# A hybrid decoder layer on one Trainium2 core: probabilities of the sliding attention folded to one square per head, scores on quarters of the array, both attentions in common visits

## The reference: what is computed

```
cb, cc, ch, cz, q, k, v, sz, mq, mz = project_in(x, pre_g, w_in)
u = cc * ch
y_conv = cb * short_conv(u_full, conv_w) * silu(cz)           # 3 taps, 384 channels
y_swa  = swa_attention(q, k_band, v_band, ...) * silu(sz)     # 6 heads, 2 kv heads, dim 64
y_mem  = mem_attention(mq, mk, mv) * silu(mz)                 # 4 heads, 256 memory tokens
y = x + rms_norm(concatenate([y_conv, y_swa, y_mem]) @ w_out, post_g)
```

## Time and profile before

| | us |
|---|---|
| median of 3 runs | 930.3 (930.17 to 930.33) |
| profiled execution | 930.49 |
| its span, first to last instruction | 928.7 |
| PE matmul busy | 890.9 (96%) |
| DVE busy | 472.8 (51%) |
| POOL busy | 485.5 (52%) |
| ACT busy | 269.0 (29%) |

### The profile page before, as it was taken

How to read it: one execution, slowest core, us unless ns; L and a number is a source line. 1 busy time by engine, 2 the same in 40 slices (tenths; PEclk the granted TensorE clock), 3 DMA queues, 4 the chain that set the end, 5 groups by cost and what they waited for, 6 DMA issues and landing times.

```text
span 928.7 us, 12297 instructions
## 1 busy us (share of the span) xinstructions
PE 890.9 (96%) x4846; PEld 717.0 (77%) x4846; DVE 472.8 (51%) x891; ACT 269.0 (29%) x726; POOL 485.5 (52%) x279
## 2 busy tenths in 40 slices
PE   1899999999999999999999999999999999999995
PEld 1799999897887777777787777777777777777784
DVE  3443247667543544674736444765535225576413
ACT  4333433331311342432311333422221124323111
POOL 1557644418667444446658444454556754444560
PEclk9999999999999999999999999999999999999998
DMA  9443421215465232212747322211822622122232
GB/s 345 182 137 125 152 70 66 69 47 196 169 200 208 99 107 91 68 68 72 268 139 267 116 91 91 68 68 48 290 76 69 216 69 78 62 75 81 84 121 90
DMA packets 40106, 114.64 MB, mean 123 GB/s; under 512 B 6001, under 2 KB 12657, under 8 KB 39633
## 3 DMA queue, kind: packets, MB, share of 16 engines
q1 hardware_dynamic: 40048, 113.86, 35.3%
HBM read 104.61 MB, written 10.25 MB: 124 GB/s over the span
## 4 chain that ended last, share of the span: by engine, by line
PE 72%; issue 2%; DVE 1%; DMA 0%; POOL 0%; POOLq 0%; DVEq 0%
PE pj L520 50%; PE pa L520 18%; PE pa L617 2%; PE pa L654 1%; DMA x_t<-in_xt 0%; DVE o_nat L1342 0%; POOL w_lo L492 0%; DVE diag L1057 0%; PE pa L541 0%; POOLq L196 0%; DVEq L196 0%; POOL w_hi L491 0%; PE pa L590 0%; PE pa L569 0%; DVE k_sb L1313 0%
## 5 line engine op out<-in xcount | busy, mean ns | idle before, releaser
L520 PE MATMUL pj<-h_hi,w_hi 128*128 128x512 f32 (+1 forms) x960 | 348.2, 363 | 1.8 <-DVE h_lo L1077 1.7
L520 PE MATMUL pj<-h_lo,w_hi 128*128 128x512 f32 (+1 forms) x960 | 339.1, 353 | 0.0
L520 PE MATMUL pj<-h_hi,w_lo 128*128 128x512 f32 (+1 forms) x960 | 338.7, 353 | 0.0
L492 POOL TENSOR_TENSOR w_lo<-w_raw,w_hi 128x1024 fp32r<-128x1024 f32 x132 | 329.2, 2494 | 11.0
L491 POOL TENSOR_SCALAR w_hi<-w_raw 128x1024 fp32r<-128x1024 f32 x132 | 146.8, 1112 | 328.1 <-PE pj L520 279.6
L520 PEld LDWEIGHTS pj<-h_hi,w_hi 128*128 128x128 f32 x960 | 181.7, 189 | 49.6 <-issue 23.7
L520 PEld LDWEIGHTS pj<-h_hi,w_lo 128*128 128x128 f32 x960 | 181.9, 190 | 24.9
L520 PEld LDWEIGHTS pj<-h_lo,w_hi 128*128 128x128 f32 x960 | 182.1, 190 | 22.5
L918 ACT ACTIVATE prob<-s_sb,nmx 128x257 f32<-128x257 f32 x96 | 47.7, 502 | 56.2 <-DVE nmx L1256 56.2
L520 PE MATMUL pa<-w_hi,y_hi 128*128 128x512 f32 x160 | 63.5, 397 | 0.0
L520 PE MATMUL pa<-w_hi,y_lo 128*128 128x512 f32 x160 | 62.4, 390 | 0.0
(11 more groups left out here) (188 smaller groups left out, 1070.3 us busy)
## 6 DMA issues: line engine op xcount, KB each, us to landing
w_raw<-in_weights SPq DMA_DIRECT2D x132, 512.0 KB, 3.3
res<-in_x_prompt SPq DMA_DIRECT2D x16, 512.0 KB, 6.8
out_y_prompt<-o_nat SPq DMA_DIRECT2D x16, 512.0 KB, 5.7
x_row<-in_x_prompt SPq DMA_DIRECT2D x12, 512.0 KB, 3.4
x_t<-in_xt SPq DMA_DIRECT2D x12, 512.0 KB, 5.4
first_rows<-in_x_prompt SPq DMA_DIRECT2D x4, 512.0 KB, 5.6
x_t<-in_xt SPq DMA_DIRECT2D x8, 256.0 KB, 5.4
mkt_s<-in_mkt SPq DMA_DIRECT2D x2, 1024.0 KB, 5.6
```

The costliest lines, as they stand in the source:

```text
L492: pool.tensor_tensor(w_lo[slot][:], w_raw[slot][:], w_hi[slot][:].bitcast(F32), ALU.subtract).then_inc(w_split, 1)
L520: return pe.matmul(out, lhsT, rhs, start=start, stop=stop)
```

## The change

- **Fold.** Of the two 128 x 128 squares of a head's probabilities (block before, own block) the masked half is zero, and the halves complement each other. `swa_norm` adds the two squares and multiplies the sum (128 columns per head) by the reciprocal. `swa_turn` then makes one transpose per head. `swa_pt` moves to DVE and multiplies each turned square by two triangular masks `seen`, a new constant of 128 x 2 x 128, loaded with the other constants; this gives `pt` its two squares again.
- **Quarters.** `swa_scores` makes two matmuls per head, each for 64 queries, on one quarter (64 rows, 64 columns) of the array, and with the 192 keys that these queries can see at most. `mem_scores` makes two per head and block too, with all 256 keys. Two PSUM banks are set to zero at the start, since parts of them are now read before they are written.
- **Common visits.** One table `ATT_S` for both scores and one `ATT_V` for both values; the transposes come 8 and 9 parts after the scores, the values 13. `swa_norm` and `mem_norm` stand at 3 and 4 parts after. M0 and M1 move up in `ROLES`, the memory tiles in quarter 0 too, and the sample's stages are earlier and closer together.
- The first gate of a quarter waits for `y_rows`, which DVE itself has counted up before.

```diff
-ROLES = ["V0", "K0", "Q0", "Q1", "Q2", "Z0", "Z1", "Z2", "M0", "M1", "Z3", "Z4"]
+ROLES = ["V0", "K0", "Q0", "Q1", "Q2", "M0", "Z0", "Z1", "Z2", "Z3", "M1", "Z4"]
...
-    return ROLES[:8] + MEM_TILES + ROLES[8:] if q == 0 else list(ROLES)
+    return ROLES[:6] + MEM_TILES + ROLES[6:] if q == 0 else list(ROLES)
...
-SW_S = {(q, i): at(q, 21, 18, i) for q in range(NQ) for i in range(NBLK)}
-SW_T = {key: s + 9 for key, s in SW_S.items()}
-SW_V = {key: s + 13 for key, s in SW_S.items()}
-MM_S = {(q, i): at(q, 38, 14, i) for q in range(NQ) for i in range(NBLK)}
-MM_T = {key: s + 7 for key, s in MM_S.items()}
-MM_V = {key: s + 10 for key, s in MM_S.items()}
-SM_S, SM_T, SM_V, SM_O = 14, 22, 27, 30
+ATT_S = {(q, i): (27, 45, 61, 77)[i] + (16 if q == 0 else 0) for q in range(NQ) for i in range(NBLK)}
+SW_T = {key: s + 8 for key, s in ATT_S.items()}
+MM_T = {key: s + 9 for key, s in ATT_S.items()}
+ATT_V = {key: s + 13 for key, s in ATT_S.items()}
+SM_S, SM_T, SM_V, SM_O = 10, 16, 19, 22
...
-                for n, h in enumerate(SCORES):
-                    r, place = HALF_OF[h // G], PLACE.index(h)
-                    if h == 2:
-
-                        pe.wait_ge(sw_s, NH * (NBLK * q + i) + 1)
-                    mm(pa[place // 2][:, (place % 2) * 2 * W:(place % 2 + 1) * 2 * W],
-                       q_sb[r, h % G, i * P:(i + 1) * P], k_sb[r, i * P:i * P + 2 * W], True, True).then_inc(sw_s, 1)
+                for pair in range(0, NH, 2):
+                    for e in range(2):
+                        for h in SCORES[pair:pair + 2]:
+                            r, place = HALF_OF[h // G], PLACE.index(h)
+                            if h == 2 and e == 0:
+
+                                pe.wait_ge(sw_s, NH * (NBLK * q + i) + 1)
+                            a, own = (place % 2) * 2 * W + e * HD, i * P + e * HD
+                            last = mm(pa[place // 2][HALF_OF[e], a:a + W + HD], q_sb[r, h % G, own:own + HD],
+                                      k_sb[r, own:own + W + HD], True, True)
+                            if e:
+                                last.then_inc(sw_s, 1)
...
                     for e in range(2):
-                        for kt in range(2):
-                            last = pe.transpose(pa[a][:, (2 * e + kt) * P:(2 * e + kt + 1) * P],
-                                                prob[:, 2 * a + e, kt * P:(kt + 1) * P], ident[:])
+                        last = pe.transpose(pa[a][:, e * P:(e + 1) * P], prob[:, 2 * a + e, 0:P], ident[:])
...
                 for tb in range(2):
-                    for hh in range(2):
-                        at_q = gr * 2 * P + tb * P
-                        last = mm(pa[3 + hh][:, tb * NM:(tb + 1) * NM], mq_sb[HALF_OF[hh], p, at_q:at_q + P],
-                                  mk_sb[HALF_OF[hh], p, :], True, True)
+                    for e in range(2):
+                        for hh in range(2):
+                            at_q = gr * 2 * P + tb * P + e * HD
+                            last = mm(pa[3 + hh][HALF_OF[e], tb * NM:(tb + 1) * NM], mq_sb[HALF_OF[hh], p, at_q:at_q + HD],
+                                      mk_sb[HALF_OF[hh], p, :], True, True)
...
-            def swa_pt(q, i):
-                for a, out in enumerate((pt[:, 0, :, 0:2, :], pt[:, 1, :, 0:2, :], pt[:, :, :, 2, :])):
-                    act.wait_ge(sw_turned, 3 * (NBLK * q + i) + a + 1)
-
-                    turned = pa[a][:].rearrange("p (e k b) -> p e k b", e=2, k=2)
-                    copy(out.rearrange("p k e b -> p e k b") if a < 2 else out, turned).then_inc(sw_pt, 1)
...
-                    need(step(dve.reciprocal(rden[:, hs], den[:, hs])))
-                    dve.tensor_tensor(prob[:, hs, 0:2 * W], prob[:, hs, 0:2 * W],
-                                      rden[:, hs].unsqueeze(2).to_broadcast([P, 2, 2 * W]), ALU.mult).then_inc(sw_p, 1)
+                    step(dve.reciprocal(rden[:, hs], den[:, hs]))
+
+                    need(step(dve.tensor_tensor(prob[:, hs, 0:W], prob[:, hs, 0:W], prob[:, hs, W:2 * W], ALU.add)))
+                    dve.tensor_tensor(prob[:, hs, 0:W], prob[:, hs, 0:W],
+                                      rden[:, hs].unsqueeze(2).to_broadcast([P, 2, W]), ALU.mult).then_inc(sw_p, 1)
+
+            def swa_pt(q, i):
+
+                for a, out in enumerate((pt[:, 0, :, 0:2, :], pt[:, 1, :, 0:2, :], pt[:, :, :, 2, :])):
+                    dve.wait_ge(sw_turned, 3 * (NBLK * q + i) + a + 1)
+                    turned = pa[a][:, 0:2 * P].rearrange("p (e t) -> p e t", e=2)
+                    dve.tensor_tensor(out if a < 2 else out.rearrange("p e k t -> p k e t"),
+                                      turned.unsqueeze(1).to_broadcast([P, 2, 2, P]),
+                                      seen[:].unsqueeze(2).to_broadcast([P, 2, 2, P]), ALU.mult).then_inc(sw_pt, 1)
...
+            for a in range(2):
+                dve.memset(pa[a][:], 0.0)
...
-                            if s == SM_S + 4:
+                            if s == SM_S + 3:
...
-                            if s == SW_S[q, i] + 4:
+                            if s == ATT_S[q, i] + 3:
                                 swa_norm(q, i)
-                            if s == MM_S[q, i] + 3:
+                            if s == ATT_S[q, i] + 4:
                                 mem_norm(q, i)
```

More of the change, by code:

```diff
@@ L155, in conv_end @@
     return CONV[q, j, len(chunks(q)) - 1]
-def at(q, base, period, i):
-    return base + period * i + (16 if q == 0 else 0)
-SW_S = {(q, i): at(q, 21, 18, i) for q in range(NQ) for i in range(NBLK)}
-SW_T = {key: s + 9 for key, s in SW_S.items()}
-SW_V = {key: s + 13 for key, s in SW_S.items()}
-MM_S = {(q, i): at(q, 38, 14, i) for q in range(NQ) for i in range(NBLK)}
-MM_T = {key: s + 7 for key, s in MM_S.items()}
-MM_V = {key: s + 10 for key, s in MM_S.items()}
-SM_S, SM_T, SM_V, SM_O = 14, 22, 27, 30
+ATT_S = {(q, i): (27, 45, 61, 77)[i] + (16 if q == 0 else 0) for q in range(NQ) for i in range(NBLK)}
[3 more added lines that the diff above has]
+SM_S, SM_T, SM_V, SM_O = 10, 16, 19, 22
 ROWS_AT = 5
@@ L193, in layer @@
 def layer(nc, x_prompt, x_sample, mem_rows, xt_d, xts_d, mt_d, weights, state_d, kt_d, cache_v, mkt_d, cache_mv, ck_old,
-          cv_old, gains, post_g, cw_d, sinks, sink_s_d, ident_d, bias_d, bias_s_d, y_prompt, y_sample, conv_p, k_p,
+          cv_old, gains, post_g, cw_d, sinks, sink_s_d, ident_d, bias_d, seen_d, bias_s_d, y_prompt, y_sample, conv_p, k_p,
           v_p, mk_p, mv_p, conv_s, k_old, k_new, v_old, v_new):
@@ L247, in layer @@
         bias = sb("bias", [P, NH, 2 * W])
+        seen = sb("seen", [P, 2, W])
         att_at = nc.sbuf_base
@@ L397, in _ @@
             sp.dma_start(bias_s[:], bias_s_d).then_inc(const_loaded, 16)
+            sp.dma_start(seen[:], seen_d).then_inc(const_loaded, 16)
             sp.dma_start(cwt[:], cw_d).then_inc(const_loaded, 16)
@@ L477, in _ @@
             sp.wait_ge(last_stored, 8 * 16)
-        N_CONST = 6 * 16
+        N_CONST = 7 * 16
         @block.gpsimd
@@ L800, in _ @@
                         for i in range(NBLK):
-                            if s == SW_V[q, i]:
+                            if s == ATT_V[q, i]:
                                 swa_values(q, i)
-                            if s == MM_V[q, i]:
                                 mem_values(q, i)
@@ L808, in _ @@
                                 mem_turn(q, i)
-                            if s == SW_S[q, i]:
+                            if s == ATT_S[q, i]:
                                 swa_scores(q, i)
-                            if s == MM_S[q, i]:
                                 mem_scores(q, i)
@@ L1019, in _ @@
                         for i in range(NBLK):
-                            if s == SW_V[q, i]:
+                            if s == ATT_V[q, i]:
                                 swa_y_hi(q, i)
-                            if s == MM_V[q, i]:
                                 mem_y_hi(q, i)
-                            if s == SW_T[q, i]:
-                                swa_pt(q, i)
                             if s == MM_T[q, i]:
                                 mem_pt(q, i)
-                            if s == SW_S[q, i]:
+                            if s == ATT_S[q, i]:
                                 swa_exp(q, i)
-                            if s == MM_S[q, i]:
                                 mem_exp(q, i)
@@ L1116, in evac @@
                         j = int(name[1])
+                        if j == 0 and c == 0 and q:
+                            dve.wait_ge(y_rows, rows_made(q - 1))
                         last = dve.scalar_tensor_tensor(out=gate[:, j, a:a + n], in0=tanh_t[:, t, 0:n], scalar=1.0,
@@ L1409, in _ @@
                         for i in range(NBLK):
-                            if s == SW_V[q, i]:
+                            if s == ATT_V[q, i]:
                                 swa_y32_of(q, i)
-                            if s == SW_V[q, i] + 1:
```

(17 more changed lines are left out.)

## The result

The changed kernel takes 921.2 us (920.7 to 921.9, 4 runs) against 930.3 for the kernel before in the same job: ratio 0.990, interval [0.989, 0.992]. It is faster by 9.1 us, where 21 were forecast, and 0.2 us outside the range. The profiled execution took 921.67 (span 919.8); before it was 930.49, so the traces have 8.8 us to explain.

The account below looks back on a forecast made before the run. The prediction took TensorE's gapless matmul stream to bound the kernel: profiled 930.5 - 26.1 (stream) + 4.8 (late turns) + 0.3 (mask) = 909.5, or 909.3 us on the median's scale; range 902 to 921.

Parts of the forecast that it names:

- The stream: TensorE's attention visits over 16 blocks: fall from 127.2 to 101.1 us, a loss of 26.1 us.
- the 0.05 for offsets: In the common score visit: 0.05 us added for offsets, within the 2.28 us expected per visit.
- Four quarters at a time: In score visits: four 64x64 quarters run at once, so sliding scores take 0.97 us instead of 1.29, memory scores 0.86 as now.
- the rival of 934: In score visits: quarters run two at a time, 29.3 us more, 934 us, slower than before; chance 0.06.
- merged visits save nothing: At common score and value visits: joining saves no entry or exit (0.40 + 0.35 each), 12 us more, 921; chance 0.05.
- Exposed weight loads: In quarter score visits: second column half's loads cost 0.1 in each of ten steps, 16 us more, 921 us; chance 0.05.
- The third pair at the turn: VectorE's normalisation in blocks 2 and 3, quarters 1 to 3: GpSimd's w_lo delays turns, 0.8 us each, 4.8 in all.
- borders at no cost: At borders of the 512-token quarters: existing TensorE waits were noted, but no added cost was put in the sum.
- GpSimd's own lateness at 0: GpSimd's weight split lacks 3.0 us from visits leaving four short memory tiles: 0 to 3 us once, taken as 0.
- the mask's 0.3: The mask's 128 KB load on SP's queue, ahead of a weight tile: 0 to 0.5 us, taken as 0.3.
- The rival with 922: VectorE at turns: a second held operation in blocks 1 to 3 makes 9 to 12 blocks wait 1.4, 922 us; chance 0.13.
- M1: Memory weight tiles M0 and M1: move up and are there before their scores, at no cost.

Follow-up runs that it names:

- experiment 8: Changed kernel with diag behind CZ2 and both turns one part later, plus scores back on halves: 907.42 us, against 901.68 with quarters.
- experiment 9: Changed kernel with diag behind CZ2 and both turns one part later, plus memory scores and values one part behind the sliding ones: 912.73 us, against 901.68.
- Experiment 2: Changed kernel with both turns one part later (9 and 10 parts behind the scores): 904.23 us, against 921.2.
- experiment 4: Changed kernel without the fold (twelve transposes, one multiply of 512 per pair, copies on ScalarE): 924.93 us, against 921.2.
- Experiments 11: Changed kernel with GpSimd waiting for the diagonals before it splits weight tile O03 at the border: 911.84 us, against 921.2.
- 12: Changed kernel with VectorE forming the next quarter's means behind tile CC2 instead of CH2: 909.0 us, against 921.2.
- 5: Changed kernel with the memory's turn alone one part later (10 parts behind the scores): 911.31 us, against 921.2.
- 6: Changed kernel with the sliding turn alone one part later, so both turns stand at 9 parts: 920.03 us, against 921.2.

## Why the prediction was right in direction and wrong in size

**The stream: right.** Forecast -26.1, measured -27.4. The score visit was put at 2.28 and is 2.20 (the 0.05 for offsets isn't there, and the entry costs a little less), the values at 2.50 and are 2.505, the turns at 0.66 and 0.88 and are 0.660 and 0.876. Four quarters at a time, read from the sample's 32-column tiles, holds in experiment 8; the rival of 934 falls with it, and experiment 9 refutes "merged visits save nothing".

**Exposed weight loads: wrong, as weighed.** The 40 records of a score visit, two tiles of each row half among them, fit into 2.20 us with no room for loads. The earlier trace rows already spoke against it: loads are busy for 717.0 us beside 890.9 of matmuls in a span of 928.7, nearly all of both on the full 128 rows. The rival's price is off too, since half of the score visit's 0.40 is 0.2 and not 0.1. The Trainium skill's sentence on weight loads ("TensorE: Matmul & The Clock Gate", "What overlaps and what doesn't" in Part 3: only with a different row group) doesn't hold for this kernel; the measurement decides.

**The third pair at the turn: right mechanism, too small.** Forecast +4.8 (0.8 in six blocks), measured +7.6 (1.51 in five). The forecast had `w_lo` hold the third multiply; it holds the add before it, so 0.43 more comes behind the hold, and `w_hi` had delayed the pair in front. It was also not covered in quarter 0, and block 3 waited in quarter 3 alone; no run was made to tell why. Experiment 2 takes it away, experiment 4 shows that the fold brings it.

**The step that failed: borders at no cost.** The prediction read that TensorE's waits lie "at the head, ..., or at the borders of the 512-token quarters" and let the gain count one for one "as long as nobody makes the stream wait", but has no term for the borders: it looked for waits only where the change adds work. Their visits cost 8.2 us more (6.8 of it longer gaps, 1.3 half clock inside the visits), and the half clock behind them 2.85, 11.05 in all, which with the 2.8 more at the turns, less the 1.3 that the stream gained and the mask's 0.3, which doesn't show, is the 12.2 us between the sum of 909.5 and the profiled 921.67. The prediction did reckon with a hold by `w_lo` at the turns, but not at the borders, and put GpSimd's own lateness at 0 since it "is in none of the four lines"; it can act through the VectorE instructions that it holds. The change takes 1.24 us of TensorE's work out of the stretch between the means and the first border: 0.88 is the memory's turn of the last block, which stood behind CH2's last matmul and now stands ahead of it, and 0.35 the second entry that the common visit for the values saves. GpSimd's 15.6 us of work there then end too late, and it holds `conv_y`, `yl_s` and at last `diag`. At the second border the stretch shrinks from 16.81 to 15.60; the `w_lo` in question ends 0.5 behind the last matmul instead of 1.1 ahead of it, and holds VectorE's copy of the last keys (`carry`) for 2.42 us, which takes 0.21 when free. Experiments 11 and 12 show the hold and its origin, 5 and 6 the stretch.

**The rival with 922.** "VectorE late at every turn" named nearly the measured time for a wrong reason, which is luck: five turns were late, not nine to twelve, and without the fold (experiment 4) the borders stayed late.

**M1.** The text on the change and the prediction say that the M0 and M1 tiles move up. M0 does; by `ROLES` M1 moves back by one tile. No wait of TensorE for it shows.

**The third border** hardly waits in either kernel (0.85 and 0.96). By the trace of the changed kernel six matmuls for the sample's output rows stand ahead of its visit, so that the stretch is 17.01 us instead of the second border's 15.60, and `w_lo` ends 0.9 ahead of the last matmul. No run was made to test this.

## What to carry to other kernels

When work is taken out of a gapless stream, measure what it stood in front of: every other engine's in-order chain up to the next meeting point must still fit into the shorter stretch, and an engine that appears in no list of waits can still arrive through instructions that it holds. Look in each queue for an early wait whose data have long been there (here 13.3 us of GpSimd, for means that could be had a tile before): moving that one line gave 12 us, more than the change itself. A gap on TensorE is charged twice if the clock falls behind it.

## What the runs showed of the hardware that was not expected

- Gaps of TensorE of 4.96 and 4.54 us were followed by a granted clock of 0.50 (1.2 GHz) for 6.8 and 3.4 us, and 1.4 us of further loss behind each visit; gaps of 2.07 us were not.
- A VectorE step of 0.27 us on 128 elements was held to 2.36 us, an add of 0.41 to 2.52, by a GpSimd instruction that had begun 0.14 and 0.19 us earlier. Even a copy with one input was: 0.21 to 2.42, by one that had begun 0.37 earlier. GpSimd's `w_hi` (1.05 us) does it too, for less (0.43 to 1.20).
- Moving the memory's turn, 0.88 us in each block, by one part (911.3 against 921.2), with the same work on every engine, changed the time by 10 us.
